# The output gates' second half moved into the first stage of a hybrid encoder layer, with 12 filler blocks per attention pair in place of 14

## Chip, cores and metric

One Trainium2 chip, one of its NeuronCores. The metric is device microseconds of one execution (lower is better). Engines are called by the profile's names: PE is TensorE (matmuls), DVE VectorE, ACT ScalarE, POOL GpSimd, SP the engine that issues most DMAs.

## What is computed

One layer of an encoder trunk, for 512 tokens of width 2048, all in float32:

```python
mod = silu(c) @ w_ada + b_ada        # 2048 -> 12288: shift1 scale1 gate1 shift2 scale2 gate2
h = rmsnorm(x, g) * (1 + scale1) + shift1
proj = h @ w_in                      # c_q 512 | c_kv 256 | k_pe 64 | q_m k_m v_m o_m 4x1024 | g_m 16
q, kv = rmsnorm(c_q) @ w_uq, rmsnorm(c_kv) @ w_ukv        # 8 attention heads
attn = softmax(rope(rmsnorm(q)) @ rope(rmsnorm(k)).T / sqrt(192)) @ v
hm = mlstm(conv(q_m, k_m), v_m, g_m) forward + backward   # 4 heads
mixed = concat(attn, sigmoid(o_m) * rmsnorm(hm)) @ w_out
x = x + gate1 * mixed
x = x + gate2 * (relu(modulate(rmsnorm(x)) @ w_ff1)^2 @ w_ff2)
```

Every large product is made of three fp32r passes over a high and a low part of each operand (`passes`, L813 to L817). ACT rounds a weight block to its high part (`split_hi`, L361), and POOL or DVE subtracts to get the low part (`split_lo`, L369; `first_lo`, L1909).

## The kernel before, in words

**Blocks.** Weights stream through a ring of four slots. A block is two k-tiles of 512 columns (512 KB), and costs PE 24 matmuls of 512 columns (2 k-tiles x 4 groups x 3 passes). Blocks have one global number `n`. SP's `load_block` (L356) waits until the low part of block n-4 is done, ACT's split until PE has finished block n-4 (`blk_done`), and POOL or DVE follow ACT.

**The start (to about 49 us).** Four tiles of `x` (128 tokens by 2048) are transposed on PE against the identity (L864 to L874), 16 transposes to a tile, and evicted by ACT to `xT`. ACT squares each tile for the norm's sum. Tiles 2 and 3 are loaded into the places of tiles 0 and 1 when these are done (L1357). The factor 1/rms of each token is turned into a row broadcast over partitions, `rstd`, by a diagonal (L397), a matmul with ones (L403) and a copy (L407).

**First stage, by quarters (to about 172 us).** A quarter q is four k-tiles of the modulated input. `shift1` and `scale1` for it are sums over 2048 rows of `w_ada`, which DVE makes in 16 steps of 1024 columns (L1871, L1874); their partition sums are 16 PE matmul records (`ada_sum`, L846). Then `ada_cols` (L1877) adds the bias (`M`), L1939 makes the gain `A1`, and `modulate` (L1883) goes through the four k-tiles: DVE multiplies `xT` by gain and `rstd` into `utmp` (L1889), ACT adds the shift and rounds (`hT[0]`, L1385), DVE makes the low part (`h_low`, L1918, two scalar and two tensor operands). PE then multiplies four blocks of w_in of that quarter (L893 to L908): two blocks of c_q (512 columns, banks 0 to 3) and two of c_kv, k_pe and gates (336 columns, banks 4 to 7). Banks 0 to 6 accumulate over all quarters; bank 7 is also needed for `ada_sum`, so DVE takes its part out after each quarter (`kv_quarter`, L1897). While PE waits it runs matmuls without use (`stay_busy`, L883). On DVE the order is written out by hand (L1922 to L1949): the 16 steps of quarter q+1 lie between the operations of quarter q.

**Fillers.** The other w_in columns (q_m, k_m in eight halves with a convolution each, then v_m in two groups of 8 blocks and o_m in two) are 64 filler blocks, `fill_at` (L73): 7 in the low-rank norms' stage (`LOW_FILLS`), then 14 in each attention pair (15 in the last), put between its dependent steps.

**An attention pair** (two heads; PE's order is `pair`, L1086): project_q, fills 0 to 2, transpose_q, fills 3 and 4, (pair 0: gate_columns), project_kv, fills 5 and 6, transpose_k, fill 7, scores, two fills, transposes of the probabilities, a fill, values, scores of head 2, two fills, transposes, a fill, values. The last pair has three fills where the others have two after each of the scores. Beside it, DVE does `norm_q` (L2116), `q_lo`, `norm_k`, softmax and low parts, the convolution taps (L2045, four per half-tile) and 32 units of the later modulation sums (`ada_unit`, L1984; their places are `ADA_AT`). A unit's 1 MB is loaded by SP into one buffer, `arawx`, once the unit before it is used (L461 to L470). The norms' powers of -1/2 are made by POOL (L755), in one queue with its splits.

**After the pairs** come the mLSTM heads, the output projection and the feed-forward part; the diff leaves them as they are.

Of the kernel before, what the change touches and what calls it, by code (L numbers as in the profile page):

```python
# [47 lines left out]
LOW_FILLS = 7  # L48
PAIR_FILLS = 14
FILLS = 8 * GB  # L50
N_PAIR = 2 * GB + LOW_FILLS
N_OUT = 2 * GB + FILLS + 4 * PAIRS
# [32 lines left out]
def kv_at(p):  # L85
    return q_at(p) + 7
# [7 lines left out]
def block_of(p, place):  # L94

    if p < 0:
# [4 lines left out]
ADA_AT = ((-1, 1), (-1, 2), (-1, 5), (-1, 6), (0, 4), (0, 8), (0, 10), (0, 13),  # L101
# [56 lines left out]
def build(nc, x, c, positions, w_ada, b_ada, norm_mix_g, w_in, b_gates, conv_w, conv_b,  # L158
# [47 lines left out]
    def over(kb, *tiles):  # L206
# [12 lines left out]
    xnat, rstd, utmp, rows0, rows1, rows2, posi, posf = over(  # L219
        0, ("xnat", [P, 2, D]), ("rstd", [P, S]), ("utmp", [P, 2, S]), ("rows0", [V_ROWS, P]),  # L220
        ("rows1", [96, P]), ("rows2", [80, P]), ("posi", [TT, P], I32), ("posf", [TT, P]))
    cq, ckv = over(16, ("cq", [P, TT, QL]), ("ckv", [P, TT, 336]))
    xsq, = over(H, ("xsq", [P, TT, D]))
# [58 lines left out]
    x_loaded = [sem("x_loaded0"), sem("x_loaded1")]  # L282
# [5 lines left out]
    n1, nm = norm_sems("norm1", "scale"), norm_sems("norm", "scale")  # L288
# [4 lines left out]
    bank_free = [sem("bank_free0"), sem("bank_free1")]  # L293
# [56 lines left out]

    def first_block(n):

        return n % 4 // 2, 2 * (n // 4) + n % 2
# [59 lines left out]
    def _(sp):  # L413
# [24 lines left out]

        for q in range(4):
            for u in range(16):  # L440
                ada_load(q, u, 512 * q, D + 512 * q, 8, araw, ada_loaded)
                if u % 4 == 3:
                    n = 4 * q + u // 4
                    g, b = first_block(n)
                    cols = 320 if g == 1 else 512
                    load_block(sp, n, n % RING, w_in3[:, KB * b:KB * b + KB, 512 * g:512 * g + cols],
                               cols, first=(q == 0))
        def fill_load(j):
            n = fill_at(j)
# [53 lines left out]
        for p in range(PAIRS):  # L503
            q_load(p)
            if p:
                pair_fills(p, 0, 2)
                mix_store(2 * p - 2)
                pair_fills(p, 2, 5)
            else:
                pair_fills(p, 0, 5)  # L510
# [6 lines left out]
            pair_fills(p, 5, PAIR_FILLS if p < PAIRS - 1 else 7)  # L517
# [34 lines left out]
        pair_fills(PAIRS - 1, 7, 10)  # L552
# [5 lines left out]
        pair_fills(PAIRS - 1, 10, PAIR_FILLS + 1)  # L558
# [25 lines left out]
        for s in range(2):  # L584
            sp.wait_ge(staged[s], 32 * 12)
# [127 lines left out]
    def _(pool):  # L713
# [46 lines left out]
        fills(0, 1, 2, 3, 4)  # L760
        power(low_ms, low_rs, 0, 0)
        fills(5, 6)
        for p in range(PAIRS):
# [48 lines left out]
    def _(pe):  # L812
# [50 lines left out]
        for t in range(TT):  # L863
            pe.wait_ge(x_loaded[t % 2], 16 * (t // 2 + 1))  # L864
            if t >= 2:
                pe.wait_ge(x_evac, 4 * (t - 1))
            if t == 1:
                pe.wait_ge(vec_cols, 1)
            for k in range(4):
                for j in range(4):  # L870
                    ft = 4 * k + j
                    ins = pe.transpose(ps[:, 4 * (t % 2) + k, j * P:(j + 1) * P],
                                       xnat[:, t % 2, ft * P:(ft + 1) * P], ident[:, :])
# [1757 lines left out]
```

## Time and profile before

| | |
|---|---|
| time, median of 3 runs | 2290.81 us (2289.87 to 2293.49) |
| the profiled execution's own time | 2286.28 us |
| its span, first to last instruction | 2284.5 us |
| PE busy | 2230.4 us (98%) |
| DVE, ACT, POOL busy | 1513.7, 828.2, 1243.8 us |
| DMA | 365.50 MB, mean 160 GB/s |
| mean granted PE clock | 0.990 of full speed |

The page says how long an engine had an instruction in work. PE's share is high partly because the kernel lets it run useless matmuls while it waits. So a stage is read from what DVE and PE wait for at its end, not from PE's share.

### The profile page before, as it was taken

The numbers are of one execution on the slowest core, as the hardware profiler recorded it, in microseconds if no ns is written. First come the engines' busy times: TensorE is split into PE (matmuls) and PEld (weight loads), VectorE is DVE, ScalarE is ACT, GpSimd is POOL, SyncE is SP. The second block draws the span as 40 slices with busy tenths as digits, with TensorE's granted clock in tenths as the row PEclk, the third lists the DMA queues.
The fourth block names the chain that finished last, engine by engine and source line by source line (L and its number), as shares of the span: only waits on it lengthen the run. The fifth ranks groups of instructions, "written<-read, shape, count | busy, mean of one in ns | idle before, by whom it ended". The sixth has DMA issues, their size and how long they took to land.

```text
span 2284.5 us, 26236 instructions
## 1 busy us (share of the span) xinstructions
PE 2230.4 (98%) x10239; PEld 1858.7 (81%) x10239; DVE 1513.7 (66%) x1506; ACT 828.2 (36%) x1108; POOL 1243.8 (54%) x528
## 2 busy tenths in 40 slices
PE   5899999999998999999999999999999999999999
PEld 4778888888887788888888888888888888888887
DVE  5969877666666377355676677677666557655756
ACT  3225454433346322333333333333333333333331
POOL 1004434343541245367777776777767677676763
PEclk8999999999999999999999999999999999999999
DMA  9875345465658485444434344343433333323342
GB/s 341 318 260 184 125 166 178 158 208 189 235 181 303 147 313 194 147 129 129 138 118 141 120 129 131 123 137 118 137 111 93 102 104 109 111 92 104 102 173 102
DMA packets 185896, 365.50 MB, mean 160 GB/s; under 512 B 15402, under 2 KB 40492, under 8 KB 183856
## 3 DMA queue, kind: packets, MB, share of 16 engines
q1 hardware_dynamic: 176992, 340.79, 45.2%
q10 hardware_dynamic: 8784, 23.07, 2.6%
q8 instruction: 80, 1.31, 0.2%
q14 instruction: 40, 0.33, 0.0%
HBM read 332.33 MB, written 31.48 MB: 159 GB/s over the span
## 4 chain that ended last, share of the span: by engine, by line
PE 88%; DVE 5%; issue 3%; DMA 2%; ACT 1%; SPq 1%; POOL 1%; DVEq 0%; ACTq 0%; POOLq 0%
PE ps L815 20%; PE ps L817 20%; PE ps L816 20%; PE ps L1273 8%; PE ps L1274 8%; PE ps L1275 8%; DVE acc L1874 2%; DMA araw<-in_w_ada 1%; PE ps L849 1%; DMA gb<-g_d 1%; PE ps L1072 1%; PE ps L886 0%; DVE accx L1997 0%; PE ps L1304 0%; SPq L434 0%
## 5 line engine op out<-in xcount | busy, mean ns | idle before, releaser
L371 POOL TENSOR_TENSOR wlo<-wraw,whi 128x1024 fp32r<-128x1024 f32 (+3 forms) x120 | 301.5, 2525 | 455.8 <-ACT whi L366 435.2
L807 POOL TENSOR_TENSOR wlo<-wq,whi 128x1024 fp32r<-128x1024 f32 x150 | 386.8, 2581 | 123.1 <-ACT whi L1766 123.1
L807 POOL TENSOR_TENSOR wlo<-wraw,whi 128x1024 fp32r<-128x1024 f32 x132 | 381.1, 2888 | 33.8 <-ACT whi L1766 33.8
L815 PE MATMUL ps<-h2T,whi 128*128 128x512 f32 x1024 | 398.6, 389 | 0.0
L817 PE MATMUL ps<-h2T,wlo 128*128 128x512 f32 x1024 | 398.4, 389 | 0.0
L816 PE MATMUL ps<-h2T,whi 128*128 128x512 f32 x1024 | 398.3, 389 | 0.0
L2476 DVE TENSOR_TENSOR yacc<-ps,yacc 128x1024 f32<-128x1024 f32 x202 | 246.3, 1219 | 215.4 <-PE ps L1275 212.8
L1273 PE MATMUL ps<-whi,ahi 128*128 128x512 f32 x840 | 326.9, 389 | 0.2 <-DVE yacc L2476 0.2
L1275 PE MATMUL ps<-whi,alo 128*128 128x512 f32 x840 | 326.8, 389 | 0.0
L1274 PE MATMUL ps<-wlo,ahi 128*128 128x512 f32 x840 | 326.8, 389 | 0.0
L1766 ACT ACTIVATE whi<-wq 128x1024 fp32r<-128x1024 f32 x150 | 159.1, 1060 | 353.1 <-PE ps L817 222.9
L807 POOL TENSOR_TENSOR wlo<-tlo,whi 128x1024 fp32r<-128x1024 f32 x60 | 146.3, 2438 | 227.0 <-ACT whi L1766 227.0
L817 PEld LDWEIGHTS ps<-h2T,wlo 128*128 128x128 f32 x1024 | 192.2, 188 | 40.2
L815 PEld LDWEIGHTS ps<-h2T,whi 128*128 128x128 f32 x1024 | 192.3, 188 | 39.7
L816 PEld LDWEIGHTS ps<-h2T,whi 128*128 128x128 f32 x1024 | 192.2, 188 | 39.6
L366 ACT ACTIVATE whi<-wraw 128x1024 fp32r<-128x1024 f32 (+2 forms) x123 | 123.3, 1017 | 205.8 <-PE ps L817 177.7
L1766 ACT ACTIVATE whi<-wraw 128x1024 fp32r<-128x1024 f32 x133 | 140.6, 1058 | 129.7 <-PE ps L1275 94.3
L1766 ACT ACTIVATE whi<-tlo 128x1024 fp32r<-128x1024 f32 x60 | 63.7, 1062 | 337.9 <-DVE tlo L2446 175.3
L1273 PEld LDWEIGHTS ps<-whi,ahi 128*128 128x128 f32 x840 | 157.7, 188 | 33.1 <-issue 0.5
L1275 PEld LDWEIGHTS ps<-whi,alo 128*128 128x128 f32 x840 | 157.7, 188 | 32.9
L1274 PEld LDWEIGHTS ps<-wlo,ahi 128*128 128x128 f32 x840 | 157.7, 188 | 32.5
L1874 DVE SCALAR_TENSOR_TENSOR acc<-araw,silc,acc 128x1024 f32<-128x1024 f32 x90 | 147.4, 1638 | 20.4 <-DMA araw<-in_w_ada 16.6
(325 smaller groups left out, 3971.5 us busy)
## 6 DMA issues: line engine op xcount, KB each, us to landing
wraw<-in_w_ff SPq DMA_DIRECT2D x136, 512.0 KB, 3.8
araw<-in_w_ada SPq DMA_DIRECT2D x128, 512.0 KB, 5.3
wq<-in_w_ff SPq DMA_DIRECT2D x120, 512.0 KB, 4.3
wraw<-in_w_in SPq DMA_DIRECT2D x72, 512.0 KB, 5.9
arawx<-in_w_ada SPq DMA_DIRECT2D x64, 512.0 KB, 4.6
wraw<-in_w_out SPq DMA_DIRECT2D x32, 512.0 KB, 6.1
xnat<-in_x ACTq DMA_DIRECT2D x4, 1024.0 KB, 8.1
xT_d<-xT ACTq DMA_DIRECT2D x1, 4096.0 KB, 13.3
```

The lines of the kernel that those rows point to most:

```text
L366: act.activation(whi[:, slot, 0:kb, 0:cols], wraw[:, slot, 0:kb, 0:cols], ACT.Copy).then_inc(hi_ready, 1)
L371: pool.tensor_tensor(wlo[:, slot, 0:kb, 0:cols], wraw[:, slot, 0:kb, 0:cols], whi[:, slot, 0:kb, 0:cols].bitcast(F), ALU.subtract).then_in ...
L807: pool.tensor_tensor(wlo[:, slot, :, :], raw, whi[:, slot, :, :].bitcast(F), ALU.subtract).then_inc(lo_ready, 1)
L815: pe.matmul(dst, lhs[0], rhs[0], start=start, stop=False)
L816: pe.matmul(dst, lhs[0], rhs[1], start=False, stop=False)
L817: return pe.matmul(dst, lhs[1], rhs[0], start=False, stop=stop)
L1273: pe.matmul(dst, a[0], w[0], start=new, stop=False, skip_group_check=True)
L1274: pe.matmul(dst, a[0], w[1], start=False, stop=False, skip_group_check=True)
L1275: ins = pe.matmul(dst, a[1], w[0], start=False, stop=i == KB - 1, skip_group_check=True)
L1766: act.activation(whi[:, slot, :, :], raw, ACT.Copy).then_inc(hi_ready, 1)
L1874: dve.scalar_tensor_tensor(tile, src, silc[:, kt:kt + 1], tile, ALU.mult, ALU.add).then_inc(ada_step, 1)
L2476: ins = dve.tensor_tensor(y, ps[:, bank:bank + 2, :], y, ALU.add)
```

## The change

- Of w_in, the last 512 columns of the output gates (heads 2 and 3) leave the fillers and become a third group (g = 2) of the first stage: a quarter has 6 blocks in place of 4 (`FIRST` = 24 in place of 16), in the order c_kv, gates, c_q (last quarter: c_q, c_kv, gates). Their sums need banks 4 to 7, which c_kv also uses. So both are taken out after each quarter: c_kv by ACT (`kv_evict`) and a DVE addition over all 1344 columns (`kv_add`), the gates by one DVE addition of 2048 columns (`og_add`; quarter 0: an ACT copy). ACT applies the sigmoid at the end (`og_gates`) and stores 1 MB.
- Fillers: 56 in place of 64; 8 in the low-rank stage in place of 7; 12 in each pair in place of 14 (last: 15). After project_q there are 2 in place of 3, after transpose_q 1 in place of 2 (last pair 2), and the last pair loses its third one after the scores. Convolution halves 5, 6, 7 move one place later (5 after `k_lo` of pair 1, 6 into its second softmax, 7 to the start of pair 2), the v groups' evictions as well, and the 32 sum units have a new table.
- The norm: `x` is transposed twice on PE, once plainly (`xT`, for the residual) and once by a matmul with a diagonal matrix that holds 1/rms (`dgx`), to `xn`. The broadcast of the factor goes, and DVE's multiplication L1889 with it: ACT makes `hT[0]` and an unrounded copy by scale and shift from `xn`, and DVE's `h_low` is a plain subtraction. All four x tiles have places of their own and are loaded at the start.
- In a quarter, `ada_sum` of the next one stands before the last block on PE, not after it.

```diff
-LOW_FILLS = 7
-PAIR_FILLS = 14
-FILLS = 8 * GB
+FIRST = 3 * GB
+LOW_FILLS = 8
+PAIR_FILLS = 12
+FILLS = 7 * GB
...
+def before_kv(p):
+    return 4 if p == PAIRS - 1 else 3
...
-ADA_AT = ((-1, 1), (-1, 2), (-1, 5), (-1, 6), (0, 4), (0, 8), (0, 10), (0, 13),
-          (1, 2), (1, 4), (1, 10), (1, 11), (1, 13), (2, "q"), (2, 2), (2, 4),
-          (2, 7), (2, 8), (2, 9), (2, 10), (2, 11), (2, 13), (3, "q"), (3, 2),
-          (3, 4), (3, "kv"), (3, 7), (3, 8), (3, 9), (3, 11), (3, 12), (3, 13))
+ADA_AT = ((-1, 1), (-1, 2), (-1, 5), (-1, 6), (0, 2), (0, 6), (0, 8), (0, 11),
+          (1, 1), (1, 2), (1, 6), (1, 8), (1, 9), (1, 11), (2, "q"), (2, 1),
+          (2, 5), (2, 6), (2, 7), (2, 8), (2, 9), (2, 10), (2, 11), (3, "q"),
+          (3, 1), (3, 3), (3, "kv"), (3, 6), (3, 7), (3, 8), (3, 9), (3, 10))
...
+    X_SETS = ((0, False), (1, False), (0, True), (1, True), (2, True), (2, False), (3, True), (3, False))
     def first_block(n):
-        return n % 4 // 2, 2 * (n // 4) + n % 2
+        q, i = n // 6, n % 6
+        return ((1, 2, 0) if q < 3 else (0, 1, 2))[i // 2], 2 * q + i % 2
...
+                    if normed:
+                        ins = pe.matmul(dst, src, dgx[:, t, :], start=True, stop=True)
+                    else:
+                        ins = pe.transpose(dst, src, ident[:, :])
...
         for q in range(4):
-            if q >= 1:
-                pe.wait_ge(ada_read, 2 * q)
-                pe.wait_ge(kv_part, q)
-                for i in range(12, 16):
-                    pe.wait_ge(ada_step, 16 * q + i)
-                    stay_busy(hT[0][:, 0, 0:P], hT[0][:, 1, :], 4 if i < 15 else 3)
-            ada_sum(q, acc[:, 2 * (q % 2):2 * (q % 2) + 2, :], 7)
             pe.wait_ge(ada_read, 2 * q + 2)
-            if q == 0:
-                pe.wait_ge(hi_ready, 1)
-                stay_busy(whi[:, 0, 0, 0:P], whi[:, 0, 1, :], 18)
-            else:
-                stay_busy(hT[0][:, 0, 0:P], hT[0][:, 1, :], 10)
-            for n in range(4 * q, 4 * q + 4):
-                g, b = first_block(n)
-                group_block(n, b, g, hin, GB, True, cols=336 if g == 1 else 512,
-                            kready=lambda kt: pe.wait_ge(h_lo, kt + 1), slot=n % RING,
-                            by_quarters=(3,) if g == 1 else ())
+            for n in range(6 * q, 6 * q + 6):
+                if q < 3 and n == 6 * q + 5:
+                    pe.wait_ge(og_evac, 4 * q + 4)
+                    for i in (14, 15):
+                        pe.wait_ge(ada_step, 16 * (q + 1) + i)
+                        stay_busy(hT[0][:, 0, 0:P], hT[0][:, 1, :], 2)
+                    ada_sum(q + 1, acc[:, 2 * ((q + 1) % 2):2 * ((q + 1) % 2) + 2, :], 7)
+                first_product(n)
...
+        def h_parts(q):
+            act.wait_ge(u_done, q + 1)
+            for k in range(4 * q, 4 * q + 4):
+                if k >= 2:
+                    act.wait_ge(h_lo, k - 1)
+                for dst in (hT[0][:, k, :], utmp[:, k % 2, :]):
+                    act.activation(dst, xn[:, k, :], ACT.Identity, bias=M[:, M_SH1 + k:M_SH1 + k + 1],
+                                   scale=A1[:, k:k + 1]).then_inc(h_hi, 1)
...
+        def kv_add(q):
+            dve.wait_ge(bank_free, kv_free(q))
+            if q >= 2:
+                dve.wait_ge(kv_part, q - 1)
+            dve.tensor_tensor(ckv[:, :, :], ckv[:, :, :], kvq[:, :, :], ALU.add).then_inc(kv_part, 1)
+        def og_add(q):
+            dve.wait_ge(blk_done, second_of(2, q) + 1)
+            dve.wait_ge(og_evac, 4 * q)
+            dve.tensor_tensor(og[:, :, :], ps[:, 4:8, :], og[:, :, :], ALU.add).then_inc(og_evac, 4)
...
         def h_low(j):
-            dve.wait_ge(h_hi, j + 1)
-            dve.scalar_tensor_tensor(hT[1][:, j, :], utmp[:, j % 2, :], M[:, M_SH1 + j:M_SH1 + j + 1],
-                                     hT[0][:, j, :].bitcast(F), ALU.add, ALU.subtract).then_inc(h_lo, 1)
+            dve.wait_ge(h_hi, 2 * j + 2)
+            dve.tensor_tensor(hT[1][:, j, :], utmp[:, j % 2, :], hT[0][:, j, :].bitcast(F), ALU.subtract
+                              ).then_inc(h_lo, 1)
...
+            kv = before_kv(p)
             project_q(p)
-            fill(0, 1, 2)
+            fill(0, 1)
             transpose_q(p)
...
-            fill(3, 4)
+            fill(*range(2, kv))
             if p == 0:
                 gate_columns()
             project_kv(p)
-            fill(5, 6)
+            fill(kv, kv + 1)
             transpose_k(p)
...
-            fill(7)
+            fill(kv + 2)
             scores(p, 0)
-            fill(8, 9, *((10,) if last else ()))
+            fill(kv + 3, kv + 4)
...
-            fill(*((12, 13, 14) if last else (11, 12)))
+            fill(kv + 6, kv + 7)
```

## Rows read from the trace of the kernel before

**Rows 1.** Stages as windows: busy us and instructions by engine, clock, DMA share, GB/s.
```profile
0.00:49.00 49.00, 22.20 (x123) 19.76 (x123) 21.62 (x23) 20.45 (x31) 6.48 (x46) 0.86 0.97 344
85.00:149.00 64.00, 58.84 (x274) 49.10 (x274) 59.14 (x62) 13.68 (x20) 0.00 (x0) 0.91 0.79 274
149.00:173.00 24.00, 23.69 (x109) 20.63 (x110) 7.38 (x13) 9.00 (x15) 4.60 (x2) 0.88 0.74 272
173.00:689.00 516.00, 512.61 (x2479) 433.33 (x2477) 373.73 (x541) 226.85 (x352) 216.71 (x93) 1.00 0.54 182
```

**Rows 2.** DVE in time, quarters: start, us, instruction, idle before it and its cause.
```profile
48.69 0.23 DVE L1880 TENSOR_TENSOR M<-ps,VT 128x4 f32<-128x4 f32 x2 [2.10 <-PE ps L849]
...
84.58 0.23 DVE L1880 TENSOR_TENSOR M<-ps,VT 128x4 f32<-128x4 f32 x2 [1.27 <-PE ps L849]
...
89.24 0.74 DVE L1889 SCALAR_TENSOR_TENSOR utmp<-xT,A,rstd 128x512 f32<-128x512 f32 x1
...
95.96 5.33 DVE L1874 SCALAR_TENSOR_TENSOR acc<-araw,silc,acc 128x1024 f32<-128x1024 f32 x4
101.21 1.22 DVE L1915 TENSOR_TENSOR wlo<-wraw,whi 128x1024 fp32r<-128x1024 f32 x1
...
108.73 0.50 DVE L1903 TENSOR_TENSOR ckv<-ckv,ps 128x336 f32<-128x336 f32 x1
...
149.02 0.23 DVE L1880 TENSOR_TENSOR M<-ps,VT 128x4 f32<-128x4 f32 x2 [1.82 <-PE ps L849]
...
172.61 0.50 DVE L1903 TENSOR_TENSOR ckv<-ckv,ps 128x336 f32<-128x336 f32 x1 [15.96 <-PE ps L817]
```

**Rows 3.** PE in time: first and last of 48 matmuls of 336 columns; the first transposes.
```profile
67.04 0.31 PE L815 MATMUL ps<-whi,hT 128*128 128x336 f32 x1
...
74.25 0.32 PE L817 MATMUL ps<-whi,hT 128*128 128x336 f32 x1
...
194.21 1.47 PE L975 MATMUL ps<-ident,cq 128*128 128x128 f32 x12
```

**Rows 4.** PE in time, the start: transposes of x, f32 matmuls of 128 columns, sums.
```profile
11.76 5.07 PE L872 MATMUL ps<-ident,xnat 128*128 128x128 f32 x32
...
41.52 0.94 PE L879 MATMUL ps<-ones,ident 128*128 128x128 f32 x6 [1.33 <-DVE acc L1874]
...
46.73 1.92 PE L849 MATMUL ps<-ones,acc 128*128 128x1 f32 x16 [2.17 <-DVE acc L1874]
```

**Rows 5.** The page's costliest groups: the DVE addition of 1024 columns from PSUM.
```profile
L2476 DVE TENSOR_TENSOR yacc<-ps,yacc 128x1024 f32<-128x1024 f32 x202 | 246.3, 1219 | 215.4 <-PE ps L1275 212.8
```

**Rows 6.** ACT, DVE and POOL in time, pair 1, from project_q's end to the rotary product.
```profile
337.79 1.46 ACT L1516 ACTIVATE qn<-ps 128x1536 f32<-128x1536 f32 x1 [5.46 <-PE ps L817]
...
339.28 1.75 DVE L2119 TENSOR_REDUCE ssq<-qn 128x8 f32<-128x1536 f32 x1 [1.47 <-ACT qn L1516]
...
347.90 4.05 DVE L2138 TENSOR_TENSOR rt<-qn,sinT 128x256 f32<-128x256 f32 x2
...
352.66 0.42 DVE L2141 TENSOR_TENSOR qr<-rt 128x256 f32<-128x256 f32 x1
...
342.91 8.75 POOL L371 TENSOR_TENSOR wlo<-wraw,whi 128x1024 fp32r<-128x1024 f32 x4
```

**Rows 7.** DVE in time, pair 0: the query norm's end, gate rows, taps, gate columns.
```profile
239.88 1.27 DVE L2105 TENSOR_TENSOR grw<-gT,gw 4x512 f32<-4x512 f32 x2
...
249.19 6.11 DVE L2045 SCALAR_TENSOR_TENSOR yc<-ps,VT,yc 128x510 f32<-128x510 f32 x8
255.22 0.22 DVE L2231 COPY gcol<-ps 128x64 f32<-128x64 f32 x1
```

**Rows 8.** DVE in time, pair 2: a sum unit right behind another, low output part.
```profile
535.35 2.61 DVE L1997 SCALAR_TENSOR_TENSOR accx<-arawx,silc,accx 128x1024 f32<-128x1024 f32 x2 [5.28 <-DMA arawx<-in_w_ada]
537.87 0.68 DVE L2210 TENSOR_TENSOR ost<-ps,ost 128x512 fp32r<-128x512 f32 x1
```

**Rows 9.** What PE waited for after 172 us: total, times, longest.
```profile
PE ps L815 <- DVE ost L2210: 2.7, 1, 2.7
```

More of the change, by code:

```diff
@@ L281, in build @@
     silc_done = sem("silc_done")
-    x_loaded = [sem("x_loaded0"), sem("x_loaded1")]
+    x_loaded = [sem(f"x_loaded{t}") for t in range(TT)]
     x_T, x_evac, kv_part = sem("x_T"), sem("x_evac"), sem("kv_part")
@@ L861, in _ @@
         pe.transpose(ps[:, 7, V_POS:V_POS + TT], posf[:, :], ident[0:TT, 0:TT]).then_inc(vec_T, 1)
[L863 to L867, printed above, removed]
+        for i, (t, normed) in enumerate(X_SETS):
+            pe.wait_ge(x_loaded[t], 16)
+            if i >= 2:
+                pe.wait_ge(x_evac, 4 * (i - 1))
+            if i == 1:
                 pe.wait_ge(vec_cols, 1)
+            if normed:
+                pe.wait_ge(x_diag, t + 1)
             for k in range(4):
@@ L1114, in pair @@
             else:
-                fill(13)
+                fill(kv + 8)
             values(p, 1)
@@ new lines, in _ @@
+        for q in range(3):
+            h_parts(q)
+            first_split(6 * q + 3)
+            first_split(6 * q + 4)
+            kv_evict(q)
+            first_split(6 * q + 5)
+            first_split(6 * q + 6)
+            if q == 0:
+                act.wait_ge(blk_done, second_of(2, 0) + 1)
+                act.activation(og[:, :, :], ps[:, 4:8, :], ACT.Copy).then_inc(og_evac, 4)
+            first_split(6 * q + 7)
+            first_split(6 * q + 8)
+        h_parts(3)
+        for n in range(FIRST - 3, FIRST):
+            first_split(n)
@@ L1697, in head @@
                                mt[:, v, :], ACT.Copy).then_inc(m_ohi, 1)
-        for n in range(2 * GB, 2 * GB + 3):
-            split(n)
-        low_copies()
-        splits(0)
+        split(FIRST)
+        kv_evict(3)
+        split(FIRST + 1)
+        act.dma_start(xT_d, xT[:, :, :]).then_inc(xT_stored, 16)
         low_squares(0)
         low_squares(1)
-        splits(1)
+        split(FIRST + 2)
         low_squares(2)
         low_squares(3)
+        splits(0)
+        og_gates()
+        splits(1)
         splits(2)
@@ L1718, in _ @@
         conv_store(0)
+        splits(7)
         act.wait_ge(xT_stored, 16)
@@ new lines, in _ @@
+            if q < 3:
+                quarter_steps(q + 1, 0, 1)
+            for i in range(4):
+                h_low(4 * q + i)
+                if i < 3 and q < 3:
+                    quarter_steps(q + 1, 2 + i)
+            if q == 3:
+                break
+            if q:
+                first_lo(6 * q + 3)
+            quarter_steps(q + 1, 5, 6)
+            first_lo(6 * q + 4)
+            quarter_steps(q + 1, 7, 8)
+            if q:
+                kv_add(q)
+            first_lo(6 * q + 5)
@@ L1950, in step @@
+            quarter_steps(q + 1, 9, 10)
+            first_lo(6 * q + 6)
+            quarter_steps(q + 1, 11, 12)
+            if q:
+                og_add(q)
+            first_lo(6 * q + 7)
+            quarter_steps(q + 1, 13, 14, 15)
+            first_lo(6 * q + 8)
+        for n in range(FIRST - 3, FIRST):
+            first_lo(n)
+        kv_add(3)
         def step(ins):
@@ L2126, in norm_q @@
                         dve.memset(qT[i][other, 2 + h, :].bitcast(F), 0.0).then_inc(zeroed, 1)
+            elif p == PAIRS - 1:
+                dve.wait_ge(v_more, 64)
+                for i in range(2):
+                    dve.memset(qT[i][ROPE:, 2, :].bitcast(F), 0.0).then_inc(zeroed, 1)
             dve.wait_ge(a_qrs, p + 1)
@@ L2336, in _ @@
         angles()
+        og_add(3)
         low_means()
```

462 lines of the change are left out of this document (245 added, 217 removed).

## The prediction

> **What bounds the kernel now.** I read the stages first [rows 1]. From 173 us to 689 us PE works 512.6 of 516 us, at the full 2.4 GHz: the fillers cover every wait of the pairs except one of 2.7 us [rows 9]. Between 85 and 149 us PE also looks busy, but there DVE works 59 of 64 us and sets the pace: its steps lie end to end from one `M` to the next, with one short wait for PE's sums [rows 2]. The three intervals between the four `M` take 100.3 us (48.69 to 149.02), the first of them 35.9 and the others 32.2 each. After the last `M`, 23.6 us pass until PE's last block of the stage is out (172.61).
>
> What PE does with such an interval: 48 matmuls of 336 columns take 74.25 - 67.04 + 0.15 = 7.4 us [rows 3], which is two blocks of c_kv. Four filler blocks run from about 172.4 to the transposes at 194.21 [rows 3], so a block of 512 columns costs 5.45 us. A quarter of four blocks is 18.3 us of useful work in 32.2 us; the other 14 us are waits and useless matmuls. That idle time in three intervals is what the change can fill. Afterwards PE's queue has hardly any slack, so a filler taken from there is time gained unless a wait appears in its place.
>
> **The first stage, part by part.** All against the profiled execution, 2286.3 us.
>
> *Moved out of the fillers:* 8 blocks of 5.45 us, 43.6 us less on PE after the stage.
>
> *DVE, quarters 1 and 2.* Removed: four multiplications L1889, 0.74 us each with 0.67 us from start to start [rows 2], 2.7 us; the old c_kv addition, 0.4 us. Added: two more low parts at 1.2 us [rows 2], 2.3 us; `kv_add`, 1344 columns, 1.5 us by the same row's rate; `og_add`, 2048 columns from PSUM, 2.3 us by twice the addition of 1024 columns, 1.22 us [rows 5]. The plain subtraction in `h_low` I take at the old price. Sum +3.0: an interval of 35.2 us, 70 for two. The extra work on ACT (four more evictions and four copies) lies beside it: ACT works 13.7 of 64 us there [rows 1].
>
> *Quarter 0* has neither addition, one extra low part only, and no modulation chain in front of PE: 35.9 - 2.7 + 1.1 for the row's terms, and about 4 us of its opening waits go, since 2 of the next quarter's steps now lie over ACT's work. I take 30 us. So the three intervals stay at about 100 us.
>
> *PE* now needs 4 x 5.45 + 7.4 = 29.2 us of each interval, plus some 2 us for `ada_sum` [rows 4]. It still fits below 35. The next quarter's sum stands before the last block, whose 5.45 us cover `M`, gain, ACT and `h_low`: PE goes through without the gap that it has now.
>
> *The tail:* after the last `M`, what is left of one block (5) and six blocks (29.2), 34.2 us for 23.6: +10.6.
>
> *The start.* Four tiles by matmul are added. An f32 matmul of 128 columns is two records; six records took 0.94 us [rows 4], so it is 0.23 us at 2.4 GHz, and twice that if the 1.2 GHz level is granted; a transpose is 5.07/32 = 0.16 [rows 4]. A normed tile costs 3.7 to 7.3 us, a plain one 2.5. The normed ones wait for DVE's diagonals, which stand behind modulation steps, and tile 2's cannot come before step 6. From there PE has two normed and two plain tiles, an eviction, 36 records of warm-up (4 us) and the sums (1.9) ahead of the first `M`, now at 48.69. I count 50 at the best clock and 54.5 at the lower level; against it, loading x at once could bring the sums' data up to 3 us sooner, which helps only if PE is not last. I take +3.7, bounds -3 and +6.
>
> DMA: a quarter loads 16 x 0.52 + 4 x 0.52 + 2 x 0.33 = 11.1 MB, 317 GB/s over 35.2 us, where the start ran at 344 [rows 1]; no term. The store of `xT` comes later but nothing reads it for 30 us. The stage then ends 3.7 + 10.6 = +14.3 us later, for 43.6 us less work behind it: **-29.3 us**.
>
> **The pairs: which cover was needed.** The filler cut after project_q and after transpose_q is 2 x 5.45 in each pair; the last loses one there (16.35 to 10.9) and two after its scores, and the low-rank stage gains one, so the stage there has more slack than now.
>
> *After project_q.* In pair 1 it ends at 337.8 (ACT's square starts), and DVE's chain ends at 353.1 [rows 6]: 15.3 us, where 16.35 us of fillers and the first transposes lie over it. With 10.9 + 0.9 us of them 3.5 us would be bare. But part of the chain is a stall: three products `rt` take 2 us each, when the like elsewhere in the chain takes 0.4 [rows 6], while POOL runs four splits that had piled up behind its power of -1/2, 8.75 us [rows 6]. With the pair's blocks closer together the pile is one of 2.4 us and two of 1.3 (c_kv's half blocks); it ends 3.5 us sooner and I take the chain at 12.3. Left bare: 0.5 us in pairs 0 and 1, 1.6 in pair 2 (taps of half 7 now stand before its norm), 2.1 in pair 3. Bounds for the four together: 0 and 16.
>
> *After transpose_q.* Pair 0 is the tight one. From the norm's end DVE does the gate rows (from 239.88), `q_lo`, the taps of a half (6.11) and the gate columns at 255.22 [rows 7]: 15.5 us in its order, whatever PE does. PE reaches the fourth c_kv matmul group 8.7 us after the transposes instead of 14.1. Bare: 6.3 us. In the others the low parts are there after 7 us and less; pair 2: 0.9.
>
> *The sum units.* One buffer: a unit behind another begins 5.28 us after it and takes 2.6 [rows 8], and the low output part behind them is already what PE waits 2.7 us for [rows 9]. The new table has units 8, 9 and 10 of pair 2 after each other, with the softmax between 8 and 9. Unit 10 then starts 5.3 us after unit 9, and `prob_lo` stands behind it with `values` on PE behind that: 6.5 us bare (0 to 9). In pair 3: 0.8.
>
> Sum of the new waits: 4.7 + 7.2 + 6.5 + 0.8 = 19.2 us, and 1.5 for a lower clock after the longer ones: **+20.7** (bounds 6 and 40).
>
> **Sum:** -29.3 + 20.7 = -8.6 us, 2277.7 us against the profiled execution. The median shown lies 4.5 us above that execution, and I expect the same of the changed kernel: 2282 us.
>
> **Rivals.**
>
> *A, the cover was mostly spare.* The pile on POOL goes and unit 10's wait is hidden by DVE's other work; only pair 0's gate chain stays bare (8 us with all of pair 0), and the start costs nothing. -43.6 + 10.6 + 8 = -25: 2266 us. For it: the waits are counted link by link with every link at its slowest. Against it: [rows 7] is one queue without gaps.
>
> *B, the cover was needed (slower).* In the pairs 9 blocks go, 49 us. If each shows as a wait, the sum is 14.3 - 43.6 + 49 = +20: 2310 us. It turns from faster to slower where more than 29 of the 49 us are bare, that is, if POOL's pile still falls on the `rt` products (+12) in all pairs and one unit's wait more appears. For it: the chain of 15.3 us against 16.35 shows cover cut to measure. Against it: the places after the scores and before transpose_k keep their fillers.
>
> *C, TensorE's f32 matmul is the new bound of the start.* The Trainium skill, "TensorE: Matmul & The Clock Gate", section Terms, says that transpose mode is four times faster for FP32. The rows here put a plain f32 matmul at 1.5 times a transpose, not four. If instead it cost 0.63 us, four times the transpose row, the four normed tiles would take 40 us, the first `M` come at about 72, 20 us later than in my sum: +12, 2303 us.
>
> *D, nothing to measure.* The gains and waits cancel within 0.2% (4.6 us, about what a measurement can tell from no change): the start at its worst bound (+2.3) and POOL's stall in half the pairs (+6). 2290 us.
>
> **How the numbers follow.** Forecast (2274 to 2286) 0.48; A 0.20; D 0.17; B 0.11; C 0.04. The range for 8 in 10 leaves out the far parts of A and of B and C: 2265 to 2296. Faster by over 0.2%: A and the forecast and a little of D, 0.69; within 0.2%: 0.17; slower: 0.14.
>
> **What would show it.** In the changed profile: first `M` near 52 us, the intervals 30, 35, 35; the last c_kv and gate additions near 187 us; no DVE wait for `araw` after the first quarter. In the pairs PE waits for `gcol` in pair 0 (6 us in all), for `qr` by 0.5 to 2 us, for the low part of pT in pair 2 (6 us). Wrong if DVE's quarter interval is above 37 us, if PE waits over 3 us for `qr` in every pair, or if the first `M` comes after 56 us.

## Result, and the profile after

The changed kernel is slower: 2301.25 us median (2299.99 to 2310.92, 5 runs) against 2290.81 (2288.96 to 2293.49) for the kernel before, measured side by side; the ratio is 1.0055, with a 95% interval of 1.0033 to 1.0077. I had forecast 2282 with a range up to 2296. The profiled execution took 2300.73 us, its span is 2298.9, 14.4 us more than before. (The medians lie 10.4 us apart: the profiled execution before was 4.5 us under its median, the one after 0.5.)

First the quarters. DVE in time, the four `M` of the changed kernel (columns as in [rows 2]; they answer to the `M` rows there):

```profile
52.09 0.23 DVE L1948 TENSOR_TENSOR M<-ps,VT 128x4 f32<-128x4 f32 x2 [7.17 <-PE ps L882]
...
86.42 0.23 DVE L1948 TENSOR_TENSOR M<-ps,VT 128x4 f32<-128x4 f32 x2 [0.90 <-PE ps L882]
...
120.96 0.23 DVE L1948 TENSOR_TENSOR M<-ps,VT 128x4 f32<-128x4 f32 x2 [0.90 <-PE ps L882]
...
156.18 0.23 DVE L1948 TENSOR_TENSOR M<-ps,VT 128x4 f32<-128x4 f32 x2 [1.59 <-PE ps L882]
```

The first comes 3.4 us later than before, and the intervals are 34.3, 34.5 and 35.2 (sum 104.1, before 100.3). The low-rank transposes, which end the stage's shadow on PE, follow at 215.39, where [rows 3] has 194.21: 21.2 us later.

Now the windows: the second and third quarter (as in [rows 1]), what follows the last `M`, and the stretch from those transposes to the first transposes of the mLSTM heads (704.97; before 690.26). The stage ends on the same work in both kernels, and the last stretch has 8 filler blocks (43.6 us) less than before.

```profile
85.00:149.00 64.00, 63.41 (x310) 54.59 (x310) 59.51 (x59) 26.62 (x37) 0.00 (x0) 0.95 0.89 306
156.20:194.00 37.80, 37.80 (x170) 32.20 (x171) 16.51 (x28) 20.88 (x48) 7.64 (x3) 0.92 0.55 199
215.39:704.97 489.58, 464.56 (x2194) 390.17 (x2192) 339.44 (x507) 205.44 (x308) 176.60 (x78) 0.96 0.52 174
```

The same stretch of the kernel before:

```profile
194.21:690.26 496.05, 491.40 (x2385) 415.86 (x2384) 354.03 (x511) 217.86 (x321) 202.20 (x86) 1.00 0.55 184
```

Before, PE was idle for 496.05 - 491.40 = 4.65 us there and at full clock. Its work was thus 491.4 us, and is 491.4 - 43.6 = 447.8 after. The changed kernel needs 489.6 for it: 25.0 us idle (489.58 - 464.56), and 16.8 us by which the same work takes longer (464.6 - 447.8). The granted clock is 0.96 here, for 1.00 before, so these 16.8 us are what the lower of the two clock levels (0.50, 1.2 GHz) costs. What PE waited for in this stretch (total, times, longest; it answers to [rows 9]):

```profile
PE ps L1131 <- DVE pT L2320: 6.9, 2, 6.4
PE ps L1072 <- DVE qr L2256: 4.1, 4, 2.3
PE ps L1123 <- DVE pr L2313: 3.7, 2, 1.9
PE ps L848 <- DVE gcol L2345: 3.0, 1, 3.0
PE ps L848 <- DVE ost L2325: 2.9, 1, 2.9
PE ps L1208 <- DVE sf L2418: 1.8, 1, 1.8
PE ps L848 <- DVE kT L2293: 1.7, 1, 1.7
```

And the clock (the column before the DMA share) around four of these waits: for the gate columns (PE idle from 273.6 to 276.6), for the low part of `pT` (567.8 to 574.2), for `qr` in pair 3 (599.4 to 600.7) and for `kT` (640.4 to 642.1):

```profile
266.00:270.00 4.00, 3.46 (x27) 2.66 (x25) 3.82 (x5) 1.37 (x2) 0.00 (x0) 1.00 0.23 43
270.00:274.00 4.00, 3.29 (x9) 2.10 (x9) 3.86 (x6) 2.25 (x2) 1.13 (x1) 0.68 1.04 351
274.00:278.00 4.00, 1.43 (x3) 1.16 (x4) 3.86 (x7) 2.30 (x5) 1.23 (x1) 0.50 0.01 4
278.00:282.00 4.00, 4.00 (x11) 3.12 (x10) 4.00 (x3) 1.04 (x2) 2.74 (x1) 0.54 0.44 117
282.00:286.00 4.00, 4.00 (x19) 3.33 (x18) 2.62 (x5) 3.12 (x4) 0.57 (x1) 1.00 1.05 360
...
568.00:572.00 4.00, 0.00 (x0) 0.00 (x0) 2.87 (x3) 0.00 (x0) 0.00 (x0) 0.97 0.82 273
572.00:576.00 4.00, 1.85 (x4) 1.50 (x5) 2.10 (x4) 0.00 (x0) 0.00 (x0) 0.50 0.79 256
576.00:580.00 4.00, 4.00 (x15) 3.33 (x14) 2.68 (x3) 0.74 (x2) 0.00 (x0) 0.67 0.36 137
580.00:584.00 4.00, 4.00 (x25) 4.00 (x24) 0.58 (x1) 0.81 (x1) 2.40 (x1) 1.00 0.79 267
...
598.00:602.00 4.00, 2.67 (x23) 2.30 (x22) 2.62 (x5) 0.60 (x1) 0.91 (x1) 1.00 0.05 18
602.00:606.00 4.00, 4.00 (x17) 3.42 (x17) 2.40 (x2) 2.12 (x4) 1.28 (x1) 0.56 0.00 0
...
640.00:644.00 4.00, 2.27 (x10) 1.59 (x9) 3.69 (x2) 1.21 (x2) 3.73 (x2) 1.00 0.95 318
```

From 278 to 282 PE is busy without a gap and gets through 11 matmuls; from 282 to 286 it gets through 19. So the price of a wait does not end with the wait.

But the price does not follow from the wait's length. Over the whole stretch the clock stands at 0.50 six times, 37.5 us in all; PE works in some 31 of them, which costs it about 16 us, and the difference above has 16.8. Five times it fell during a wait or within 2 us behind one, for 3.4 to 6.8 us: at the waits of 2.3, 2.9, 6.4 and 1.3 us and at the last two of 1.9 and 1.8. The wait of 1.7 us for `kT` was followed by none. And the longest low stretch, 10.2 us around the wait for the gate columns, began at about 271.4 us, 2.2 us ahead of that wait, while PE was at work; before it PE had two waits of 0.5 and 0.3 us and 16 matmuls of 4 columns.

Where the waits sit on DVE shows best in pair 2, the sum units and the low part of `pT` (DVE in time):

```profile
550.05 2.61 DVE L2108 SCALAR_TENSOR_TENSOR accx<-arawx,silc,accx 128x1024 f32<-128x1024 f32 x2 [4.95 <-DMA arawx<-in_w_ada]
...
558.09 5.63 DVE L2108 SCALAR_TENSOR_TENSOR accx<-arawx,silc,accx 128x1024 f32<-128x1024 f32 x2
569.10 2.61 DVE L2108 SCALAR_TENSOR_TENSOR accx<-arawx,silc,accx 128x1024 f32<-128x1024 f32 x2 [5.37 <-DMA arawx<-in_w_ada]
571.62 2.48 DVE L2320 TENSOR_TENSOR pT<-ps,pT 128x512 fp32r<-128x512 f32 x4
```

Units 9 and 10 stand in a row: DVE waits 5.4 us for the second's load while the transposed probabilities (on PE from 560.39) are long there.

### The profile page after: what moved, and what is told of

Its sections match the earlier page's. It is cut to its first block, busy times and chain, and to the rows that moved or that the text cites. A ratio compares the mean times of both kernels' runs of the same rounds, so it can differ in the third digit from the quotient of the medians.

```text
span 2298.9 us, 26418 instructions
## 1 busy us (share of the span) xinstructions
PE 2236.6 (97%) x10302; PEld 1867.1 (81%) x10302; DVE 1497.6 (65%) x1506; ACT 859.6 (37%) x1152; POOL 1221.5 (53%) x521
## 4 chain that ended last, share of the span: by engine, by line
PE 84%; DVE 7%; DMA 3%; issue 2%; ACT 1%; SPq 1%; POOL 1%; ACTq 0%; DVEq 0%; POOLq 0%
PE ps L848 18%; PE ps L850 18%; PE ps L849 18%; PE ps L1327 8%; PE ps L1325 8%; PE ps L1326 8%; DVE accx L2108 2%; DMA arawx<-in_w_ada 1%; PE ps L882 1%; PE ps L909 1%; DMA araw<-in_w_ada 1%; DVE acc L1993 1%; DVE rt L2253 1%; DMA wraw<-in_w_in 1%; DVE pr L2313 0%
## 5 line engine op out<-in xcount | busy, mean ns | idle before, releaser
L395 POOL TENSOR_TENSOR wlo<-wraw,whi 128x1024 fp32r<-128x1024 f32 (+3 forms) x112 | 277.6, 2490 | 484.8 <-ACT whi L390 454.1
L848 PE MATMUL ps<-hT,whi 128*128 128x512 f32 x384 | 150.7, 392 | 0.0
```

The costliest lines, as they stand in the source:

```text
L395: pool.tensor_tensor(wlo[:, slot, 0:kb, 0:cols], wraw[:, slot, 0:kb, 0:cols], whi[:, slot, 0:kb, 0:cols].bitcast(F), ALU.subtract).then_in ...
L848: pe.matmul(dst, lhs[0], rhs[0], start=start, stop=False)
```

## Experiments

Each time is given as the ratio to the kernel before on the same chip, with its 95% interval; the changed kernel stands at 1.0055. The intervals are 2 to 5 us to each side, so two changed kernels can be told apart by the whole time from about 5 us; below that the parts of the trace are compared, and they are one profiled execution each.

**Useless matmuls during the waits.**

```diff
+        def idle(bank, count):
+            for _ in range(count):
+                pe.matmul(ps[:, bank, :], hT[0][:, 0, 0:P], hT[0][:, 1, :], start=True, stop=True)
...
+            if p == 0:
+                idle(4, 14)
...
+            if p >= 2:
+                idle(6, 10 if p == 2 else 6)
             pe.wait_ge(a_qr, p + 1)
```

> The changed kernel with useless matmuls of 512 columns (0.227 us each at 2.4 GHz) in front of the places where PE waits in the pairs: 14 before project_kv of pair 0 (where it waited 3.0 us for the gate columns), 10 and 6 before the qr transposes of pairs 2 and 3, 13 before the second scores and 26 before the second transposes of pair 2 (waits of 2.9 and 6.4 us), 7 before the first scores of pair 3 (1.7 us). No wait is removed, PE only has something in work during them. Theory (the clock): of the 37 us that the pairs gave back, some 16 are matmuls at the 1.2 GHz level behind the new waits; kept busy, PE stays at 2.4 GHz and 13 to 16 us go: 2286 to 2289 us, the granted clock of the pairs at 0.99 to 1.00 in place of 0.96. Rival (the chains): DVE's and POOL's chains set the pace of the pairs, so a faster PE only comes to the next wait sooner: 2297 to 2302 us. A third outcome, that the useless matmuls push real work back, would give up to 17 us more, 2318.

Ratio 1.0052 (1.0036 to 1.0069), the rival's figure in the whole time. But the pairs' stretch did change:

```profile
218.15:702.64 484.49, 472.69 (x2270) 397.94 (x2268) 339.57 (x507) 205.48 (x308) 177.81 (x78) 0.99 0.52 176
```

484.5 us for 489.6. Over the 447.8 us of work stand 11.8 idle, 17.3 of useless matmuls (76 x 0.227) and 7.6 at the lower level, for 25.0, 0 and 16.8. The lower clock does hang on PE having no work: 9.2 us of it went. But idle and useless time together rose by 4.1: the place of the `pT` wait took 9.5 us (26 useless matmuls, 5.9 us, and 3.6 idle) for 6.4, so DVE's row sets when the wait ends, and a PE that comes sooner waits longer. In this execution the first stage took 2.8 us more (transposes at 218.15), which hid most of the rest. So each side was half right: the clock recovered as the theory said (0.99 granted), the whole time did not.

**Another table of units.**

```diff
-          (1, 1), (1, 2), (1, 6), (1, 8), (1, 9), (1, 11), (2, "q"), (2, 1),
-          (2, 5), (2, 6), (2, 7), (2, 8), (2, 9), (2, 10), (2, 11), (3, "q"),
+          (1, 1), (1, 2), (1, 5), (1, 6), (1, 8), (1, 9), (1, 11), (2, "q"),
+          (2, "kv"), (2, 5), (2, 6), (2, 7), (2, 8), (2, 10), (2, 11), (3, "q"),
...
-            if p in (1, 3):
-                ada_sum(4 if p == 1 else 6, accx, 7)
+            if p:
+                ada_sum(3 + p, accx, 7)
```

> The changed kernel with another table of the sum units: pair 1 takes 7 in place of 6 (one more before its first softmax), pair 2 has 7 with none at its place 9, so that no two stand in a row between its second softmax and the low part of pT, and the second later sum is made right after transpose_q of pair 2, as in pairs 1 and 3. Theory: the 6.4 us wait for pT's low part (units back to back at one 5.4 us load each) and the half clock behind it (about 3.5 us) go: 8 to 10 us less, 2291 to 2293 us. Rival: the unit moved into pair 1 and the earlier sum put the same wait there: 2297 to 2303 us.

Ratio 1.0062 (1.0049 to 1.0075), as the rival had it. The 6.4 us wait is gone, and the head transposes come at 698.10, 6.9 us sooner. Three others grew: the gate columns' from 3.0 to 3.9 us, `kT` in pair 3 from 1.7 to 4.1, and there are 3.7 us for ACT's sigmoid behind the last filler, in place of the `pr` waits. From the heads on this execution took 1598.6 us where the changed kernel took 1593.9, with clock 0.93 against 0.96 from 705 to 800 us. A gain in the pairs is partly given back behind them, at the lower clock (see the end of the next part).

**The vector loads first.**

```diff
+        act.wait_ge(vec_loaded, 16 * 13)
+        for t in range(2, TT):
+            act.dma_start(x_tile(t), x[t * P:(t + 1) * P, :]).then_inc(x_loaded[t], 16)
```

> The changed kernel, with the loads of x tiles 2 and 3 issued only once the small vector loads have landed, behind ACT's first square. Theory: the four 1 MB loads at the front are what moved the positions' arrival from 10.6 to 15.2 us, with every later step of the start behind it; the first M comes 3 to 4.5 us sooner (48 to 49 us) and the time is 3 to 4.5 us less, 2297 to 2298 us. Rival: PE's and ACT's chain of 128 transposes and evictions with the warm-up is what ends last, and tiles 2 and 3 now come later: the first M stays at 52 us or comes later, 2300 to 2303 us.

Ratio 1.0073 (1.0060 to 1.0086): the rival. The first transposes moved from 15.52 to 10.61 us, the first `M` from 52.09 to 53.87. The early chain was not on the path.

**Gate columns ahead of the taps.**

```diff
-                conv_taps(1)
                 dve.wait_ge(g_colT, 1)
...
+                conv_taps(1)
```

> The changed kernel with one swap on DVE in pair 0: the copy of the gate columns (0.2 us) ahead of the taps of convolution half 1 (6.1 us) in place of behind them. Theory: PE's wait of 3.0 us and the stretch at 1.2 GHz behind it (about 5 us of work lost from 264 to 320 us) go: 6 to 8 us less, 2293 to 2295 us. Rival: the gate columns' transposes on PE come so late that DVE now waits for them and the taps and the key norm's chain move back: the wait turns up at transpose_k and the gain is under 2 us, 2299 to 2303 us.

Ratio 1.0062 (1.0049 to 1.0075), yet locally it worked: PE has no wait for `gcol` any more, one of 0.6 us for `kT` instead, and from the query transposes of pair 0 to the probability transposes of pair 1 it takes 155.5 us for 159.5. The low clock around that place did not go wholly: 3.4 us at 0.50 are left of 10.2, with no wait for `gcol` there. Pairs 2 and 3 gave back 2.5 of the 4, and the time behind the pairs 2.2 more.

**No useless matmuls ahead of the first sum.**

```diff
-        for i in range(8, 14):
-            pe.wait_ge(ada_step, i)
-            for _ in range(3):
-                pe.matmul(ps[:, 7, 0:P], ident[:, :], ones[:, :], start=True, stop=True)
```

> The changed kernel without the 18 useless f32 matmuls ahead of the first ada_sum, which lie between the last eviction of xn (46.1 us) and the sum (50.2 us), where DVE's 16 steps have long been done. Theory: they are on the path that sets the first M: it comes 4 us sooner (48 us) and, as the blocks of quarter 0 follow from it on PE, the time is about 4 us less, 2296 us. Rival: without them PE enters the sum and quarter 0 at 1.2 GHz, or the weight blocks' high and low parts come last: first M at 48 but the second M where it was (86 us), 2299 to 2302 us.

Ratio 1.0077 (1.0059 to 1.0095): the rival. First `M` at 48.51, second at 88.22, behind the 86.42 of the changed kernel.

**Half of the gate products left out.** (So half of the output gates of heads 2 and 3 is not summed: the run prices PE's work, it is no kernel to use.)

```diff
+                if g == 2 and not (kt % 4 in (0, 3)):
+                    continue
```

> The changed kernel with half of PE's gate products left out (of each quarter's four k-tiles the first and the last are multiplied, 24 matmuls of 512 columns for 48; so the output gates of heads 2 and 3 lack half of their sum). DVE, ACT, POOL and the loads are as before. Theory: quarter 0 was set by PE's own row of blocks and not by DVE (34.3 us where I had 30): it falls by 4 to 5 us, to about 30, while the other two, where DVE sets the pace, stay at 34.5 and 35.2; the last quarter falls by 5.4; 2290 us in all. Rival: DVE or the loads set all three, the intervals stay within 1 us and only the last quarter's 5.4 us go: 2295 us.

Ratio 1.0042 (1.0027 to 1.0057), some 3 us less than the changed kernel, which its interval does not tell from nothing: nearer the rival's 2295 than the theory's 2290, and above both. The intervals are 33.2, 35.9 and 35.8. In quarter 0 PE now waits 2.5 us for DVE's step 14:

```profile
78.91 0.70 PE L918 MATMUL ps<-hT 128*128 128x512 f32 x2 [2.52 <-DVE acc L1995]
80.23 1.22 PE L918 MATMUL ps<-hT 128*128 128x512 f32 x2 [0.63 <-DVE acc L1995]
```

So with 5.45 us less work on PE the quarter is 1.1 us shorter: DVE's row is right behind PE's there. The pairs took 490.8 us, with one wait of 9.8 us for `pT` in place of 6.4.

**All waits of DVE's row together.** The gate columns as above, the second later sum after transpose_q of pair 2, a table that is not the one tried above, and, new here, a unit between the key norm and the low part of `kT` (`k_lo`):

```diff
-          (1, 1), (1, 2), (1, 6), (1, 8), (1, 9), (1, 11), (2, "q"), (2, 1),
-          (2, 5), (2, 6), (2, 7), (2, 8), (2, 9), (2, 10), (2, 11), (3, "q"),
-          (3, 1), (3, 3), (3, "kv"), (3, 6), (3, 7), (3, 8), (3, 9), (3, 10))
+          (1, 1), (1, 2), (1, 4), (1, 5), (1, 6), (1, 8), (1, 9), (1, 11),
+          (2, "kv"), (2, 4), (2, 5), (2, 6), (2, 8), (2, 10), (2, 11), (3, "q"),
+          (3, 1), (3, 3), (3, "kv"), (3, 5), (3, 6), (3, 7), (3, 8), (3, 10))
...
             norm_k(p)
+            ada(p, before_kv(p) + 1)
             k_lo(p)
```

> The changed kernel with the two DVE edits that worked locally, gate columns ahead of the taps in pair 0 and the second later sum after transpose_q of pair 2, and a new table: pair 1 takes 8 units, one of them in the 10 us of DVE idle time between the key norm and k_lo; pairs 2 and 3 have one there too, and none in front of their second softmax's successors in a row (pair 3's in front of the second softmax, where DVE waited 6.5 us for its load, is gone). Theory (each new wait has a place in DVE's row and goes when a unit is moved out of it): the waits for gcol, qr in pair 2, ost, pT and pr go, some 17 us with 9 to 12 us of half clock behind them: 2276 to 2282 us. Rival (the pairs lack cover as a whole, 8 blocks less, and a wait removed is paid at the next link): 2293 to 2299 us.

2276.74 us, ratio 0.9953 (0.9939 to 0.9968): the theory's figure, and below the kernel before. The stretch of the pairs and its waits:

```profile
214.36:679.50 465.14, 454.30 (x2194) 382.98 (x2192) 341.17 (x507) 205.47 (x308) 177.95 (x78) 0.99 0.54 183
```

```profile
PE ps L848 <- DVE kT L2289: 4.0, 2, 3.1
PE ps L1072 <- DVE qr L2252: 2.8, 4, 1.3
PE ps L1204 <- DVE sf L2413: 1.8, 1, 1.8
```

465.1 us for 489.6: 10.8 idle in place of 25.0 and 6.5 at the lower level in place of 16.8. The waits for `gcol`, `ost` and `pr` are gone, that for `pT` is 0.6. The two edits that were run alone had shown nothing of this in the whole time: what they took away came back, in whole or in part, at the next late link or behind the pairs. But the third, the unit ahead of `k_lo` with its table, was never run alone. So it is shown that the three together remove these waits; that none of them would have done most of it alone is not shown.

**The same without the useless matmuls ahead of the first sum.** (Both edits as above.)

> Both of the former: the new table and DVE order, and no useless matmuls ahead of the first sum. If the two gains are independent: 4 us below the kernel with the table alone, 2272 to 2278 us, and below the kernel before (2287). If the earlier first M only moves the same waits forward: equal to the kernel with the table alone within 1.5 us.

2276.64 us, ratio 0.9948 (0.9935 to 0.9961): no gain. First `M` at 48.51, second at 86.87 (with them 52.41 and 86.91). What the 4 us are lost to, on DVE and on POOL beside it:

```profile
48.51 0.23 DVE L1940 TENSOR_TENSOR M<-ps,VT 128x4 f32<-128x4 f32 x2 [3.41 <-PE ps L882]
48.77 0.31 DVE L2023 SCALAR_TENSOR_TENSOR A<-M,VT 128x4 f32<-128x4 f32 x1
49.00 2.20 DVE L1982 TENSOR_SCALAR acc<-araw,silc 128x1024 f32<-128x1024 f32 x1
51.24 3.28 DVE L1985 SCALAR_TENSOR_TENSOR acc<-araw,silc,acc 128x1024 f32<-128x1024 f32 x1
```

```profile
47.45 5.97 POOL L395 TENSOR_TENSOR wlo<-wraw,whi 128x672 fp32r<-128x672 f32 x3 [17.92 <-ACT whi L1422]
```

The two steps take 2.20 and 3.28 us beside POOL's splits, where they took 0.74 and 1.28 in the changed kernel: 3.5 of the 4 us.

**Loads of w_ada ahead of the weight blocks.** (On top of the three edits, the "kernel with the table alone".)

```diff
+                if q == 1 and u == 7:
+                    for n in (4, 5, 6):
+                        first_load(n)
+                    continue
                 n = 6 * q + {1: -2, 3: -1, 7: 0, 11: 1, 13: 2, 15: 3}.get(u, -6 * q - 1)
-                if n >= 0:
+                if n >= 0 and not (q == 1 and u < 7):
                     first_load(n)
```

> The kernel with the new table and DVE order, and one more edit, on SP: the loads of the first two weight blocks of quarter 1 come behind the first eight loads of w_ada of that quarter, not among them. There SP waited 13 us for POOL's first low part, with the w_ada loads behind it, the DMA engines at half load from 40 to 50 us and full from 50 to 90. Theory (the loads set quarter 0's end): the second M, which stood at 86.4 to 88.2 us in all runs with full gate work, comes 1 to 3 us sooner, the time 1 to 3 us below 2276.7. Rival (DVE's and PE's rows of quarter 0 set it): no change at the second M, 2276 to 2278 us.

2272.9 us, ratio 0.9930 (0.9917 to 0.9944), the fastest of all. From 40 to 50 us in the kernel with the table alone, and in this one; then its second and third `M`:

```profile
40.00:50.00 10.00, 9.10 (x82) 8.87 (x81) 3.82 (x3) 8.09 (x16) 2.67 (x2) 1.00 0.51 186
```

```profile
40.00:50.00 10.00, 9.10 (x82) 8.87 (x82) 3.50 (x3) 7.53 (x14) 3.21 (x3) 1.00 1.06 388
```

```profile
84.83 0.23 DVE L1948 TENSOR_TENSOR M<-ps,VT 128x4 f32<-128x4 f32 x2 [0.90 <-PE ps L886]
...
119.01 0.23 DVE L1948 TENSOR_TENSOR M<-ps,VT 128x4 f32<-128x4 f32 x2 [1.60 <-PE ps L886]
```

The DMA engines no longer stand half idle, and the second and third `M` come 2.1 and 2.5 us sooner (from 86.91 and 121.53): the theory. The whole time fell by more, 0.23% or some 5 us against the table alone, which the two intervals only just tell from nothing. In the profiled executions 1.6 us of it are the first stage; the pairs took 460.4 us for 465.1 (9.3 idle, 3.3 for the lower clock), and the time behind them 2.2 more. Why the pairs gained is not shown.

**The same without the useless matmuls ahead of the first sum.**

> The same with the useless matmuls ahead of the first sum left out. That edit moved the first M by 4 us and the second not at all. If the loads were what held the second M, it now follows the first: 83 to 84 us, 2272 to 2274 us in all. If not, 2276 to 2278 us.

2275.67 us, ratio 0.9950 (0.9937 to 0.9964): the second `M` at 86.69, so it did not follow and the time is the other outcome; POOL's splits held DVE as above (2.21 and 3.26 us), and PE waited 3.4 us for the low part and did quarter 0's first matmuls at the lower level. With the useless matmuls in, the first `M` comes when these splits are over; they are best left in.

**Useless matmuls at the waits that are left.** Four, 6 and 8 of them, by the same `idle`.

> The kernel with the new table and DVE order, with useless matmuls (4, 6 and 8 of 512 columns, 0.9, 1.4 and 1.8 us) where PE still waits: the qr transposes of pairs 2 and 3 and the first scores of pair 3. Theory (the clock): these waits of 0.9 to 3 us are behind most of the half clock that is left in the pairs (some 5 us), so 2 to 4 us go: 2273 to 2275 us. Rival: waits as short as these cost no clock, or the clock falls elsewhere: 2276 to 2278 us.

2275.98 us, ratio 0.9947 (0.9933 to 0.9961). The pairs took 460.0 us for 465.1, but the time from the heads on was 1599.4 us, where the kernel with the table alone took 1596.3; in the whole time nothing can be told.

**The kernel before, with the same kind of edits.** (A table of its own, as its fillers have other places.)

> The kernel before (gates in the fillers, 14 fillers per pair), with the same kind of edits as the new table and DVE order: gate columns ahead of the taps, second later sum after transpose_q of pair 2, pair 1 takes 7 units, one of them between the key norm and k_lo, and none in a row in front of pair 2's out_lo. Theory (the edits only pay where the fillers are too few): PE waits in the pairs for 4.7 us in all, of which one wait of 2.7 us is for a unit, so at most 3 us go: 2284 to 2288 us, and the moved gates are then worth some 9 us on their own. Rival (the edits shorten the pairs whatever their cover, the moved gates are worth nothing): 2270 to 2276 us.

2285.87 us, ratio 0.9985 (0.9976 to 0.9994): the theory. In its pairs the clock stands at 1.00 throughout. The edits are worth 0.15% with the old cover and 1.0% with the new one (1.0055 to 0.9953). With DVE's row in order on both sides, the change is worth 0.9953 / 0.9985 = 0.9968, some 7 us faster (by the two intervals, 3 to 11). The change has several parts, the gates, the norm, the loads of `x` and the place of `ada_sum`; no run has one of them without the others, so this is the worth of all together.

## Why the prediction was wrong

The sum was -8.6 us against the profiled execution, the spans gave +14.4. The step that failed is the term of 1.5 us for the lower clock in the pairs, which measured 16.8; the first stage, 6.9 us too short in the sum, comes second. Point by point:

- **First `M`** (+3.7): 3.4 measured. Right. Rival C falls too: a normed tile took 3.74 us and a plain one 1.91 (the rows below, both at a granted clock of 1.00), so the f32 matmul is twice a transpose beside it, and 1.5 times the slower ones of [rows 4], not four times. Rival C's own sum was short as well: 64 matmuls at 0.63 in place of 0.23 us are 25.6 us more, not 20.

```profile
39.71 3.74 PE L909 MATMUL ps<-dgx,xnat 128*128 128x128 f32 x32
43.28 1.91 PE L911 MATMUL ps<-ident,xnat 128*128 128x128 f32 x16
```

- **Intervals** (30, 35, 35): 34.3, 34.5, 35.2. Quarter 0 failed by 4.3. I took DVE's old row and struck "about 4 us of its opening waits"; what stayed, 35.9 - 2.7 + 1.1 = 34.3, is what was measured. Three rows meet there within 1 to 2 us: PE's own (its first product at 56.8, five blocks, useless matmuls and the sum), DVE's (half the gate work: 1.1 us less) and the loads (moved forward: 2.1 us less). I checked the loads against DVE's pace for the later quarters (317 GB/s) and found "no term"; in quarter 0 they ran at 382 to 386 GB/s from 60 us on, because SP had stood 13.2 us behind POOL's low part (8.7 in the kernel before) with the w_ada loads queued behind it. That wait was the one I should have priced: SP's queue gets more weight blocks ahead of them.
- **The tail** (+10.6): 14.0. What is left behind the last `M` was summed at full clock (34.2 us) and took 37.6; the window from 156.2 to 194 has 0.92, so 3 us are the lower level, as in [rows 1] before. The last gate addition stands at 193.9, where I had 187.
- **After project_q** (4.7) and **after transpose_q** (7.2): `qr` 4.1; `gcol` with `gT` and `qT` 3.8. **Sum units of pair 2** (6.5): 6.4, in the place and for the reason given. **Pair 3** (0.8): 5.9 (`kT`, `pr`, `pT`), missed: a unit in front of its second softmax waited 6.5 us for its load. In all 20.4 us of new idle time against 19.2. That the sum fits is partly luck: the gate chain was 3.4 us under its figure and pair 3 was 5.1 over.
- **The clock** (1.5): 16.8. This is the step that failed. I priced the lower level for "the longer ones" at a tenth of the waits, and the rows show low stretches at all but one of the waits of 1.3 us and more, and one that began ahead of its wait. The only such wait in the pairs of the kernel before, 2.7 us, left the clock at 1.00, and I took it for the rule. The run with useless matmuls took 9.2 of the 16.8 us away without removing a wait, the run with the three edits took 10.3 together with the waits. With this term at its size the same sum is +6.7, and with the first stage's 6.9 us +13.6. The term alone carries the forecast of 2282 past the end of the range (2297). The 4.5 us that I added for the median were an offset of one execution; the changed kernel's was 0.5.

So rival B came true in its outcome and not in its mechanism: 20.4 of the 49 us were bare, less than its 29, and what decided was what a bare microsecond costs: 37.2 / 20.4 = 1.8. The Trainium skill, "TensorE: Matmul & The Clock Gate", section "Part 1: The HAM clock gate", says that for modelling "the ramp penalty is <1% of a typical kernel span". In this stretch the rows agree: 16.8 of 2298.9 us is 0.7%. Over the whole execution they do not: a granted clock of 0.985 leaves out 1.5% of the span (before: 0.990, 1.0%). And the 16.8 us are twice the gain that I forecast.

The time from the heads on grew by 2 to 5 us in most runs (1593.9 us in the changed kernel, 1596.1 to 1599.4 in those with the new table). The granted clock goes with it. The first 100 us from the heads on, in the changed kernel and in the last of those with the new table:

```profile
704.97:804.97 100.00, 92.73 (x472) 76.71 (x473) 47.56 (x119) 48.70 (x105) 21.84 (x15) 0.97 0.59 210
```

```profile
675.55:775.55 100.00, 94.12 (x456) 77.22 (x457) 47.64 (x119) 47.62 (x104) 18.11 (x13) 0.90 0.56 198
```

Four more, with the granted clock of these 100 us and the time from the heads on: 0.97 and 1594.2 us in the kernel before, 0.95 and 1596.0 in the same with its edits, 0.92 and 1596.3 with the three edits, 0.91 and 1598.6 with the first other table. It isn't that the pairs end sooner: the kernel before with its edits reaches the heads 0.9 us before the one without, and takes 1.8 us longer behind them.

What stays open: what makes the same wait cost clock in one execution and not in another, whether another spread of the fillers over the pairs would do better, and what each part of the change and the unit ahead of `k_lo` are worth alone; none of this was tried.

## What to carry to other kernels

When work is moved out of a row of fillers, price the uncovered microseconds together at nearly two each, not at one: in idle time and in stretches at the lower clock around it. New idle time and lower clock together came to 1.8 times the new idle time in the changed kernel, 2.0 with the three edits and 1.7 with the loads moved as well. It is a price for the sum only; a single wait of 1.3 us cost between nothing and 3.4 us. Then do not stop at the sum of the waits; each has a place in the other engine's row, and here reordering that row (a late load, a small copy behind a long operation, units in a row) was worth 1.0%, some 23 us, when the two edits that were run alone showed nothing in the whole time. Test such edits together as well as singly.

## What the runs showed of the hardware

- The same wait, 1.3 us for `qr` in pair 3, was followed by 6.8 us at a granted clock of 0.50 in the changed kernel and with the gate columns moved, by 3.4 us with the three edits and with the loads moved, and by none with the first other table and with half of the gate products. A wait of 2.7 us left the clock at 1.00 in the kernel before, one of 3.1 us (`kT`) with the three edits.
- The clock also fell while PE was at work: at about 271.4 us, with no wait of over 0.6 us in the 20 us before.
- With useless matmuls at the waits the granted clock of the pairs went from 0.96 to 0.99.
- Two DVE operations of 1024 columns took 2.20 and 3.28 us beside POOL's splits, and 0.74 and 1.28 without them.
- At a granted clock of 1.00, 16 f32 matmuls of 128x128 took 3.74 us and 16 transposes 1.91.
- Dropping 4.3 us of useless matmuls moved the first `M` by 3.9 us and the second not at all (52.41 and 86.91; 48.51 and 86.87).
